# The projection of a small per-layer input, computed in an earlier stage and loaded in the last one

## What is computed

```python
def _expert_choice(u, w_router, w_gate, w_up, w_down):
    aff = jax.nn.softmax((tok @ w_router).astype(jnp.float32), axis=-1)
    cap = max(1, CAPACITY_FACTOR * T // N_EXPERTS)
    gate, idx = lax.top_k(aff.T, cap)
    ...
# _forward, at the end of the layer
u2 = _rmsnorm(h, w['g_ffn'][i])
h = h + _expert_choice(u2, w['w_router'][i], w['w_exp_gate'][i], w['w_exp_up'][i], w['w_exp_down'][i])
ple_gate = jax.nn.sigmoid(h @ w['w_ple_gate'][i] + w['b_ple_gate'][i])
h = h + ple_gate * (p[i] @ w['w_ple_proj'][i])
return _rmsnorm(h, w['g_final'])
```

## Time and profile before

| | |
|---|---|
| Median of 3 runs | 3293.35 us (3291.61 to 3296.46) |
| The profiled execution | 3291.5 us |
| its span, first to last instruction | 3289.5 us |
| mean granted TensorE clock | 0.914 of 2.4 GHz |
| busy: TensorE, VectorE, ScalarE, GpSimd | 2752.9, 1652.2, 1262.2, 300.9 us |
| DMA | 515.88 MB, mean 157 GB/s |

### The profile page before, as it was taken

How to read it: one execution, slowest core, us unless ns; L and a number is a source line. 1 busy time by engine, 2 the same in 40 slices (tenths; PEclk the granted TensorE clock), 3 DMA queues, 4 the chain that set the end, 5 groups by cost and what they waited for, 6 DMA issues and landing times. The chain is left out here.

```text
span 3289.5 us, 42094 instructions
## 1 busy us (share of the span) xinstructions
PE 2752.9 (84%) x15560; PEld 2359.9 (72%) x15560; DVE 1652.2 (50%) x2158; ACT 1262.2 (38%) x1791; POOL 300.9 (9%) x346
## 2 busy tenths in 40 slices
PE   3999999894677279687996991799999999998696
PEld 2789888683556157576784880799999999997575
DVE  5100000523888687540664228577777777776324
ACT  4111111322566445331442110355555555554222
POOL 1000000100001200020110000001111010101122
PEclk6999999897889699898998995699999999999798
DMA  8412120644310334573875540478878787885312
GB/s 272 115 64 89 71 85 39 201 145 124 92 34 11 89 95 127 162 259 106 293 252 186 191 153 2 149 237 250 252 234 259 245 251 239 248 246 156 110 40 101
DMA packets 446372, 515.88 MB, mean 157 GB/s; under 512 B 18280, under 2 KB 386808, under 8 KB 445400
## 3 DMA queue, kind: packets, MB, share of 16 engines
q1 hardware_dynamic: 414304, 390.10, 38.5%
q0 software_dynamic: 31968, 124.44, 11.9%
HBM read 392.65 MB, written 121.83 MB: 156 GB/s over the span
## 5 line engine op out<-in xcount | busy, mean ns | idle before, releaser
L2033 DVE TENSOR_TENSOR ex_w_lo<-ex_w_raw,ex_w_hi 128x2048 fp32r<-128x2048 f32 x195 | 443.9, 2291 | 142.9 <-ACT ex_w_hi L1990 142.9
L2122 PE MATMUL ex_ps_u<-ex_x,ex_w_hi 128*128 128x384 f32 x2048 | 411.1, 341 | 5.1 <-DVE ex_w_lo L2033 5.1
L1990 ACT ACTIVATE ex_w_hi<-ex_w_raw 128x2048 fp32r<-128x2048 f32 x195 | 370.4, 1909 | 0.8
L2122 PEld LDWEIGHTS ex_ps_u<-ex_x,ex_w_hi 128*128 128x128 f32 x2048 | 348.7, 189 | 6.1 <-issue 5.5
L2122 PEld LDWEIGHTS ex_ps_u<-ex_x,ex_w_lo 128*128 128x128 f32 x2048 | 265.5, 191 | 0.6
L2141 PE MATMUL ex_ps_d<-ex_w_hi,ex_h 128*128 128x512 f32 x768 | 265.8, 400 | 0.0
L2122 PE MATMUL ex_ps_u<-ex_x,ex_w_lo 128*128 128x192 f32 x2048 | 265.5, 272 | 0.0
L354 DVE TENSOR_TENSOR w_lo<-w_raw,w_hi 128x2048 fp32r<-128x2048 f32 x15 | 34.3, 2290 | 404.1 <-ACT w_hi L322 404.1
L328 ACT ACTIVATE stage<-ps 128x512 f32<-128x512 f32 (+1 forms) x102 | 55.9, 548 | 414.9 <-PE ps L376 359.5
L2141 PE MATMUL ex_ps_d<-ex_w_lo,ex_h 128*128 128x512 f32 x512 | 202.9, 396 | 0.0
L2141 PEld LDWEIGHTS ex_ps_d<-ex_w_hi,ex_h 128*128 128x128 f32 x768 | 144.6, 188 | 35.0
(11 more groups left out here) (380 smaller groups left out, 5188.0 us busy)
## 6 DMA issues: line engine op xcount, KB each, us to landing
ex_w_raw<-in_w_exp_gate SPq DMA_DIRECT2D x64, 1024.0 KB, 5.2
ex_w_raw<-in_w_exp_up SPq DMA_DIRECT2D x64, 1024.0 KB, 6.1
ex_w_raw<-in_w_exp_down SPq DMA_DIRECT2D x64, 1024.0 KB, 6.5
w_raw<-in_w_in SPq DMA_DIRECT2D x15, 1024.0 KB, 5.7
mg_w_raw<-in_w_ssm_up SPq DMA_DIRECT2D x24, 512.0 KB, 5.7
mg_g_raw<-g_d SPq DMA_DIRECT2D x24, 512.0 KB, 7.1
xbcT_d<-stage POOLq DMA_DIRECT2D x5, 1536.0 KB, 5.6
cv_raw<-xbcT_d POOLq DMA_DIRECT2D x10, 768.0 KB, 5.7
```

Of the source, the lines that this page charges most:

```text
L1990: act.activation(w_hi[:, j % CUT], w_raw[:, j % RAW], ACT.Copy).then_inc(w_hi_done, 1)
L2033: dve.tensor_tensor(w_lo[:, j % CUT], w_raw[:, j % RAW], w_hi[:, j % CUT].bitcast(F32), ALU.subtract).then_inc(w_split, 1)
L2122: last = pe.matmul(ps_u[:, j % 2, m, 0:wide * C], w[:, s, k, cols], x[:, k, 0:wide].rearrange("p a c -> p (a c)"), start=i == 0, stop=i == ...
```

## The change

`p` is laid out features first by the host, [128, 2, 1536]. `choose_tokens` gets it, loads it and `w_ple_proj` whole, splits both (the rounding on ScalarE, the rest on GpSimd) and computes the product of all 12 tiles in 24 halves of 6 matmuls. ScalarE copies each half from PSUM into one of four buffers, and SP stores it in a new tensor `ple_d` in device memory. `embed_and_norm` loads the tile of `ple_d` (128 x 1024) where it loaded the tile of `p` (128 x 256), has no `ps_p`, no `w_ple_proj` and no transposes of `p`, and `mix` reads the product from `hp`.

```diff
-def choose_tokens(nc, logits, token_ids, slot_numbers, ident, index, gate):
+def choose_tokens(nc, logits, token_ids, slot_numbers, ident, index, gate, pT, w_ple_proj, ple_d):
...
+    KP, HB = PLE // P, D // BLK
+    HALVES = [(t, c) for t in range(TT) for c in range(HB)]
...
+        p_raw, w_raw = sb("p_raw", [P, KP, T]), sb("w_raw", [P, KP, D])
+        p_hi, p_lo = sb("p_hi", [P, KP, T], F32R), sb("p_lo", [P, KP, T], F32R)
+        w_hi, w_lo = sb("w_hi", [P, KP, D], F32R), sb("w_lo", [P, KP, D], F32R)
+        e_out = sb("e_out", [P, 4, BLK])
...
+        ps_e = ctx.enter_context(nc.psum_tensor("ch_ps_e", [P, 2, BLK], F32))
...
@@ sync, behind the three constants
+            sp.dma_start(p_raw[:], pT).then_inc(p_in, 16)
+            sp.dma_start(w_raw[:], w_ple_proj.rearrange("(k p) d -> p k d", p=P)).then_inc(wp_in, 16)
+            for n, (t, c) in enumerate(HALVES):
+                sp.wait_ge(e_copied, n + 1)
+                sp.dma_start(ple_d[t][:, c * BLK:(c + 1) * BLK], e_out[:, n % 4]).then_inc(e_out_done[n % 4], 16)
+            for done in e_out_done:
+                sp.wait_ge(done, 16 * len(HALVES) // 4)
+
+        @block.gpsimd
+        def _(pool):
+            pool.wait_ge(p_hi_done, 1)
+            pool.tensor_tensor(p_lo[:], p_raw[:], p_hi[:].bitcast(F32), ALU.subtract).then_inc(p_split, 1)
+            pool.wait_ge(wp_hi_done, 1)
+            pool.tensor_tensor(w_lo[:], w_raw[:], w_hi[:].bitcast(F32), ALU.subtract).then_inc(wp_split, 1)
...
@@ scalar, between the copy into value and the wait for value_ready
+            act.wait_ge(p_in, 16)
+            act.activation(p_hi[:], p_raw[:], ACT.Copy).then_inc(p_hi_done, 1)
+            act.wait_ge(wp_in, 16)
+            act.activation(w_hi[:], w_raw[:], ACT.Copy).then_inc(wp_hi_done, 1)
+            for n in range(len(HALVES)):
+                act.wait_ge(e_full, n + 1)
+                if n >= 4:
+                    act.wait_ge(e_out_done[n % 4], 16 * (n // 4))
+                act.activation(e_out[:, n % 4], ps_e[:, n % 2], ACT.Copy).then_inc(e_copied, 1)
...
@@ tensor, between the transposes of logits and the wait for place_ready
+            for n, (t, c) in enumerate(HALVES):
+                if n == 0:
+                    pe.wait_ge(wp_hi_done, 1)
+                    pe.wait_ge(p_hi_done, 1)
+                if n >= 2:
+                    pe.wait_ge(e_copied, n - 1)
+                terms = [(v, w, k) for v, w in ((p_hi, w_hi), (p_lo, w_hi), (p_hi, w_lo)) for k in range(KP)]
+                for i, (v, w, k) in enumerate(terms):
+                    if n == 0 and i == KP:
+                        pe.wait_ge(p_split, 1)
+                    if n == 0 and i == 2 * KP:
+                        pe.wait_ge(wp_split, 1)
+                    last = pe.matmul(ps_e[:, n % 2], v[:, k, t * P:(t + 1) * P], w[:, k, c * BLK:(c + 1) * BLK], start=i == 0, stop=i == len(terms) - 1)
+                last.then_inc(e_full, 1)
...
@@ embed_and_norm
-    KA = KT + KP
+    KA = KT
...
-        hp = sb("hp", [P, 2, D + PLE])
+        hp = sb("hp", [P, 2, 2 * D])
...
-        ps_p = ctx.enter_context(nc.psum_tensor("fi_ps_p", [P, HB, BLK], F32))
...
-                sp.dma_start(rows[:, KT:KA, cols], w_p[:, :, cols]).then_inc(w_in[c], 16)
...
-                    pool.dma_start(hp[:, s, D:D + PLE], p[tile]).then_inc(landed[s], 16)
+                    pool.dma_start(hp[:, s, D:2 * D], ple_d[tile]).then_inc(landed[s], 16)
...
-                dve.tensor_tensor(z[:, c], sig[:, c], ps_p[:, c], ALU.mult).then_inc(mixed, 1)
+                dve.tensor_tensor(z[:, c], sig[:, c], hp[:, s, D + c * BLK:D + (c + 1) * BLK], ALU.mult).then_inc(mixed, 1)
...
-                for ps, ks in ((ps_g, range(KT)), (ps_p, range(KT, KA))):
-                    terms = [(v, w, k) for v, w in ((a_hi, w_hi), (a_hi, w_lo), (a_lo, w_hi)) for k in ks]
-                    for i, (v, w, k) in enumerate(terms):
-                        last = pe.matmul(ps[:, c], v[:, s, k], w[:, k, cols], start=i == 0, stop=i == len(terms) - 1)
+                terms = [(v, w, k) for v, w in ((a_hi, w_hi), (a_hi, w_lo), (a_lo, w_hi)) for k in range(KT)]
+                for i, (v, w, k) in enumerate(terms):
+                    last = pe.matmul(ps_g[:, c], v[:, s, k], w[:, k, cols], start=i == 0, stop=i == len(terms) - 1)
...
-        "x": both("x_prompt", "x_sample", D), "p": both("p_prompt", "p_sample", PLE),
+        "x": both("x_prompt", "x_sample", D), "p": both("p_prompt", "p_sample", PLE).reshape(T, PLE // P, P).transpose(2, 1, 0),
```

More of the change, by code:

```diff
@@ L1802, in choose_tokens @@
         hot_ready, picked, picked_read = sem("hot_ready"), sem("picked"), sem("picked_read")
+        p_in, wp_in, p_hi_done, wp_hi_done, p_split, wp_split = (sem(n) for n in ("p_in", "wp_in", "p_hi_done", "wp_hi_done", "p_split", "wp_split"))
+        e_full, e_copied, e_out_done = sem("e_full"), sem("e_copied"), [sem("e_out%d" % s) for s in range(4)]
         block = ctx.enter_context(nc.Block())
@@ L2143, in _, with embed_and_norm @@
                                     last.then_inc(*((d_full, 1) if g == 0 else (unit_done, 2)))
-def embed_and_norm(nc, h_d, p, w_ple_gate, b_ple_gate, w_ple_proj, g_final, ident, y_tiles):
-    HB, KP = D // BLK, PLE // P
-    KA = KT + KP
+def embed_and_norm(nc, h_d, ple_d, w_ple_gate, b_ple_gate, g_final, ident, y_tiles):
+    HB = D // BLK
+    KA = KT
     NORMS, STEPS = ((0, TT - 2), (TT - 2, TT)), 7
@@ L2175, in _ @@
             w_g = w_ple_gate.rearrange("(k p) d -> p k d", p=P)
-            w_p = w_ple_proj.rearrange("(k p) d -> p k d", p=P)
             for c in range(HB):
@@ L2198, in _ @@
                 pool.dma_start(hp[:, s, 0:D], h_d[s]).then_inc(landed[s], 16)
-                pool.dma_start(hp[:, s, D:D + PLE], p[s]).then_inc(landed[s], 16)
+                pool.dma_start(hp[:, s, D:2 * D], ple_d[s]).then_inc(landed[s], 16)
             with pool.Fori(0, TT // 2 - 1) as it:
@@ L2233, in _ @@
                     split_hi(0, 0)
-                act.wait_ge(w_in[c], 32)
+                act.wait_ge(w_in[c], 16)
                 cols = slice(c * BLK, (c + 1) * BLK)
@@ L2266, in add_bias, with mix @@
                 dve.tensor_tensor(z[:, c], ps_g[:, c], bias[:, c * BLK:(c + 1) * BLK], ALU.add).then_inc(biased, 1)
-            def mix(n, c):
+            def mix(s, n, c):
                 dve.wait_ge(gated, HB * n + (c + 1))
-                dve.tensor_tensor(z[:, c], sig[:, c], ps_p[:, c], ALU.mult).then_inc(mixed, 1)
+                dve.tensor_tensor(z[:, c], sig[:, c], hp[:, s, D + c * BLK:D + (c + 1) * BLK], ALU.mult).then_inc(mixed, 1)
             def keep(s, n, tile):
@@ L2288, in _ @@
                     add_bias(n, 0)
-                    mix(n, 0)
+                    mix(s, n, 0)
                     split_lo(1 - s, n + 1)
                     add_bias(n, 1)
-                    mix(n, 1)
+                    mix(s, n, 1)
                     keep(s, n, bass.ds(n, 1))
@@ L2313, in _ @@
             add_bias(TT - 2, 0)
-            mix(TT - 2, 0)
+            mix(0, TT - 2, 0)
             split_lo(1, TT - 1)
             add_bias(TT - 2, 1)
-            mix(TT - 2, 1)
+            mix(0, TT - 2, 1)
             keep(0, TT - 2, slice(TT - 2, TT - 1))
@@ L2321, in _ @@
             add_bias(TT - 1, 0)
-            mix(TT - 1, 0)
+            mix(1, TT - 1, 0)
             norm_rows(4, 8)
             add_bias(TT - 1, 1)
-            mix(TT - 1, 1)
+            mix(1, TT - 1, 1)
             norm_rows(8, TT - 2)
@@ L2383, in encoder_layer @@
     g = dram("g_d", 2, KT, NB, P, BLK)
+    ple = dram("ple_d", T, D)
     with nc.sbuf_tensor("u_hi", [P, KT, T], F32R) as u_hi_now, nc.sbuf_tensor("u_lo", [P, KT, T], F32R) as u_lo_now:
@@ L2394, in encoder_layer @@
         project_out(nc, m_hi, m_lo, x, w_out, g_ffn, w_router, ident, logits, tiles(h), tiles(u2))
-        choose_tokens(nc, logits, token_ids, slot_numbers, ident, index, gate)
+        choose_tokens(nc, logits, token_ids, slot_numbers, ident, index, gate, p, w_ple_proj, tiles(ple))
         run_experts(nc, u2, index, gate, w_exp_gate, w_exp_up, w_exp_down, ident, h)
@@ L2398, in encoder_layer @@
     y_tiles = [tiles_of(y_prompt)[i] for i in range(TT1)] + [tiles_of(y_sample)[i] for i in range(TT - TT1)]
-    embed_and_norm(nc, tiles(h), p, w_ple_gate, b_ple_gate, w_ple_proj, g_final, ident, y_tiles)
+    embed_and_norm(nc, tiles(h), tiles(ple), w_ple_gate, b_ple_gate, g_final, ident, y_tiles)
 def kernel(**inputs):
```

## The result

The kernel after takes 3301.64 us, median of 10 runs (3298.28 to 3303.77), against 3293.68 (3291.61 to 3296.46, 10 runs) for the kernel before: a ratio of 1.0022, 95% interval 1.0013 to 1.0032. The change makes the kernel slower by 8 us. The prediction was 3302.0.

A forecast was written before the change was run, and what follows sets the result against it. The last stage's loop was taken as bound by a chain of waits through each tile's load and second half, the choosing stage by VectorE. 13.7 - 5.0 + 0 = +8.7 us gave 3302 us, range 3291 to 3313.

The forecast's parts named there:

- the loop: Last stage's loop over ten tiles: +1.37 us per tile, +13.7 us in all, bounds +7 and +24.
- The clock, +1.95 per tile: Last stage's loop: TensorE's pause grows from 1.6 to 4.0 us, its clock falls, transposes and second half slow by 1.95.
- The load, +1.05 per tile: Last stage's loop: a tile's load grows from 640 to 1024 KB and lands 1.05 us later, bounds 0.95 and 1.4.
- What is taken out, -1.63 per tile: Last stage's loop: 6 second-half matmuls (1.37 us) and two of ten transposes (0.26) leave the path.
- The start of the last stage, -5.0: Before the loop: smaller weight copy and subtraction, shorter first halves and turn, landing +0.3; -5.0 us, bounds -3.5 and -6.5.
- The choosing stage, 0: Stage choosing the experts' tokens: added loads, splits, matmuls and stores hide beside VectorE's rounds of max and replace; 0 us.
- the prediction's own sign of being wrong: Wrong if the loop's clock reads 1.00, the load takes over 5 us, or the choosing stage grows over 1 us.
- The rival of the clock that holds: Last stage's loop keeps full clock: -0.58 us per tile and -5 at the start, 3282.5 us, faster; chance 0.10.
- The rival of a fall that costs half: Last stage's loop: the clock's fall costs only 0.9 us per tile, 3291.5 us, no change; chance 0.10.
- The rival of GpSimd's subtractions against VectorE's rounds: Choosing stage: GpSimd's new subtractions hold up VectorE, at worst for all 12.9 us, 3315 us; chance 0.05.

The follow-up runs named there:

- e1_fill16: Kernel after plus 16 discarded matmuls between each tile's first half and the next tile's transposes, TensorE's loop written out; 3283.56 us, ratio 0.9972 to before.
- e10_both: Kernel after with three slots for loaded tiles instead of two, and the choosing stage's load of p waiting until the three constants landed; 3241.18 us, ratio 0.9836.
- e1b_fill8: Kernel after plus 8 discarded matmuls ahead of each next tile's transposes, TensorE's loop written out; 3295.00 us, ratio 1.0008.
- e7_h_alone: Kernel after with a separate semaphore for the product's load, so the transposes wait for h only and the mix for the product; 3280.82 us, ratio 0.9964.
- e4_small_load: Kernel after, but the loop loads only 32 of 128 partitions of the product's tile (128 KB); 3291.01 us, ratio 0.9999.
- e8_h_alone_fill8: Kernel after with a separate semaphore for the product's load and 8 discarded matmuls ahead of the transposes; 3272.37 us, ratio 0.9937.
- e3_last_only: Last stage of the kernel after with the choosing stage of before; another tensor's tiles are loaded in place of the product's; 3305.47 us, ratio 1.0029.

## Why the prediction was right

The median came out 0.4 us from the forecast. That it is so near is luck: the loop was forecast 2.3 us too dear and the start 0.3 too dear, the choosing stage 1 to 1.5 too cheap, and these cancel in part. The mechanism is not luck: each large term can be set beside a measured one.

*The clock, +1.95 per tile, bounds 1.4 and 2.6.* Measured 1.74 by e1_fill16, and the clock fell in all ten tiles. The pause was 4.0 us, as worked out. The step that carried it was that matmuls of the same shape behind 4.58 and 2.84 us of pause took 5.12 and 5.35 us; the lower bound of 1.4 was nearer than the upper, which came from a start after a long idle time. The rows were chosen one-sidedly, though. The same stretch of the scan stage has more bursts of 8 matmuls, these two among them:

```profile
1153.23 1.94 PE L1145 MATMUL sc_ps<-sc_wide,sc_x_in 128*64 128x512 f32 x8 [2.83 <-DVE sc_wide L964]
...
1162.78 3.50 PE L1145 MATMUL sc_ps<-sc_wide,sc_x_in 128*64 128x512 f32 x8 [2.18 <-DVE sc_wide L964]
```

A pause of 2.83 us cost nothing there and one of 2.18 cost 1.6, so the kernel before already showed that the outcome is mixed at such pauses. At 4.0 us it was not, which no row of before could tell but the one of 4.58. Nor did the loss fall where I put it: I expected 7 to 8 us for the 24 matmuls of the second half, and they take 5.9 to 7.4, since up to 0.9 us of the loss is in the transposes. In two tiles of the ten it cost 2.8 (turn to bias 9.4), in the others 1.3 to 1.6.

*The load, +1.05 per tile.* Measured 4.47 against 3.46: 1.01.

*What is taken out, -1.63 per tile.* Turn to bias with the clock at 1.00 went from 8.19 to 6.61: 1.58. Sum per tile: -1.58 + 1.01 + 1.74 = +1.17, against +1.14 measured and +1.37 forecast. Of the 2.3 us between 13.7 and 11.4, 2.1 are the clock's term. For the mix, which reads the product from SBUF now, I had given nothing, and it takes 0.70 us as before; my reason was a misreading, since 0.70 us for 512 elements is 1.37 ns each and not the 1.07 of the subtraction.

*The start of the last stage, -5.0.* Measured -5.3, with two errors that nearly cancel. Up to the first matmul it is -1.64 (it comes 23.05 us after the stage's first instruction, and came 24.69 after it), where I had -2.0. The weights are there 13.7 us after the stage's start and not 13.2, 0.5 later where I took 0.3; copy and subtraction take 3.62 and 4.42 us instead of 4.48 and 5.49, as worked out. From the first matmul to the bias of (0, 1) it is 13.7 us and was 17.4, 3.7 less where I had 3.0. The 0.7 is in the first 24 matmuls, which still run partly at the lower clock: they take 7.30 us, and took 8.05. In the other runs with this last stage they take 7.06 to 7.88, so this part of the gain varies from run to run.

*The choosing stage, 0.* This step was wrong, by 1 to 1.5 us: in the two traces compared the stage takes 113.7 us up to the experts' first instruction and took 112.7. By 1.07 us more, it just meets the prediction's own sign of being wrong (more than 1 us). I had found 12 us of spare time for TensorE, and that was so: its last matmul of the projection ends at 2035.0, as worked out, and it then idles 15.2 us before the place transposes. The new loads I had placed behind the three constants without asking whether these would land later. They did, and here VectorE's whole stage waits for the last of them. e10_both gave it back in the trace.

*The rival of the clock that holds* would have been 3282.5, and e1_fill16 is that case made by hand: 3283.6. Its two terms, -0.58 per tile and -5 at the start, measured -0.53 and -4.9 in that run.

*The rival of a fall that costs half* did not come: all ten fell. But e1b_fill8 and e7_h_alone show its second form, that some pauses do not cost at all: at 2.0 to 3.3 us the clock fell in 8 and 6 of ten tiles.

*The rival of GpSimd's subtractions against VectorE's rounds* is out: max and replace took the same 1.04 and 1.02 us beside 11.2 us of GpSimd, which I had put at 12.9, and VectorE's whole stretch is as long with it as without. The Trainium skill's rule that I had set beside this rival (SBUF — State Buffer, on the ports that VectorE and GpSimd share: outside the two-port modes an instruction with one SBUF input does not contend) agrees with that. What the Trainium skill says in TensorE: Matmul & The Clock Gate, section on HAM oscillation, the trace bears out in the main: with the wait of 4.0 us the clock fell in every tile. That each tile's work begins cold is so in seven tiles; in the three others the transposes began at full clock and the fall came while they ran. And with waits of 2.0 to 3.6 us (e1b_fill8, e7_h_alone, e4_small_load) it did not fall every time.

## What to carry to other kernels

Taking work off an engine that also waits for a load in every round makes that wait longer, and TensorE's clock can make the wait cost a second time: here 4.0 us of pause cost 1.74 more behind it, per tile. Look at the wait before the work: with one more slot the same change is worth 34.7 us and not -8. And when loads are added to a queue, ask which small transfer in front of them somebody is waiting for: here the small one came 1.4 us later.

## What was not expected of the hardware

- A pause of 2.17 us kept the clock and one of 1.97 lost it (e1b_fill8); one of 3.33 kept it and one of 2.60 lost it (e7_h_alone). In pauses of up to 1.8 us it held in every tile (before, e1_fill16, e8_h_alone_fill8), and also in one of 2.49 (first tile of before); in those of 3.8 to 4.6 it fell in all ten (after).
- The fall can come after the work has begun again: the transposes behind a pause of 4.16 us ran 0.6 us at full clock before it (after).
- Shortening a pause from 4.0 to 2.2 us won back two falls of ten. Half of the filler is worth 5 us, all of it 17 (each median against the kernel before in its series).
- Of two transfers queued one behind the other on GpSimd's queue, the first landed 3.7 us after its issue, though 512 KB stood behind it; the second 4.5 after its own (after). Waiting for the pair cost 1.3 us against waiting for the first.
- Loads of the same size from two tensors of the same shape landed 4.47 (after) and 4.85 us (e3_last_only) after their issue. Why is open.
- The small load of the slot numbers landed 1.4 us later in the mean with 2.5 MB queued behind it (eight runs against three), and at its old time once they waited for it (e10_both).
